# Norm and routing of an expert stage: tokens on the partitions, first maxima by a running count, ranks in bf16

## What is computed

```python
h = rmsnorm(x, g_moe[l])                      # x * rsqrt(mean(x*x) + EPS) * g
g_prob = softmax(xt @ w_rg + b_rg);  p_grp, grp = lax.top_k(g_prob, 1)
e_logits = (xt @ w_re + b_re).reshape(T, N_GROUPS, EXPERTS_PER_GROUP)
e_in = jnp.take_along_axis(e_logits, grp[:, :, None], axis=1)[:, 0]
top_p, top_i = lax.top_k(softmax(e_in), 2)
weights = p_grp * top_p / jnp.sum(top_p, axis=-1, keepdims=True)
hid = silu(xb @ w_gate[e]) * (xb @ w_up[e]);  y = hid @ w_down[e] * w
```

## Time and profile before

| | |
|---|---|
| median of three runs | 1666.05 us |
| the profiled execution | 1660.06 us, its span 1658.3 us |
| granted TensorE clock, mean | 0.944 |
| TensorE busy | 1446.1 us, 87% of the span |
| VectorE busy | 735.5 us, 44% |
| ScalarE busy | 549.2 us, 33% |
| moved from HBM | 371.92 MB, 225 GB/s over the span |

### The profile page before, as it was taken

The page is one execution under the profiler, slowest core; times in us unless marked ns, Lnnn a source line. Parts: engine busy times, 40 slices in busy tenths (PEclk is TensorE's granted clock), DMA queues, the critical chain, the costliest instruction groups (busy, mean ns, idle before and its releaser), DMA issues.

```text
span 1658.3 us, 23155 instructions
## 1 busy us (share of the span) xinstructions
PE 1446.1 (87%) x10239; PEld 1189.1 (72%) x10239; DVE 735.5 (44%) x1072; ACT 549.2 (33%) x678; POOL 2.9 (0%) x8
## 2 busy tenths in 40 slices
PE   7998999877667667576699999999999999999998
PEld 6696888653323223232488888999988888899997
DVE  2555624331101001011487756666466665666642
ACT  2461522311101001001345734444343573453431
POOL 0000000000000000000000000000000000000000
PEclk9997999979988889889899999999999999999999
DMA  6542128449999999999844216556542421655540
GB/s 216 212 175 102 51 102 344 166 165 421 421 421 421 421 421 422 420 421 421 310 153 153 103 53 214 182 163 227 193 163 103 153 102 67 220 171 174 208 153 26
DMA packets 129804, 374.51 MB, mean 226 GB/s; under 512 B 9271, under 2 KB 54631, under 8 KB 105127
## 3 DMA queue, kind: packets, MB, share of 16 engines
q1 hardware_dynamic: 125735, 370.71, 58.7%
q0 software_dynamic: 528, 2.04, 0.4%
q10 hardware_dynamic: 3440, 0.25, 0.2%
HBM read 371.92 MB, written 1.06 MB: 225 GB/s over the span
## 4 chain that ended last, share of the span: by engine, by line
PE 64%; DMA 15%; DVE 9%; SPq 6%; ACT 3%; issue 2%; DVEq 0%; ACTq 0%
PE bank L595 32%; PE bank L1125 7%; DMA ring<-in_w_exp_up 7%; SPq L481 6%; DMA SZ<-in_w_exp_up 5%; PE bank L619 4%; PE bank L951 3%; DVE parts L1576 3%; PE bank L813 3%; PE bank L913 2%; PE bank L641 2%; PE bank L573 2%; PE bank L978 2%; DMA SZ<-in_w_exp_down 2%; DMA ring<-in_w_out 1%
## 5 line engine op out<-in xcount | busy, mean ns | idle before, releaser
L595 PE MATMUL bank<-hnr,parts 128*128 128x256 f32 x4032 | 495.1, 284 | 0.8 <-DVE parts L1576 0.8
L595 PEld LDWEIGHTS bank<-hnr,parts 128*128 128x128 f32 x4032 | 487.9, 192 | 6.1 <-issue 5.1
L1576 DVE TENSOR_TENSOR parts<-ring,parts 128x2048 fp32r<-128x2048 f32 x136 | 306.2, 2287 | 130.8 <-ACT parts L1219 129.2
L1219 ACT ACTIVATE parts<-ring 128x2048 fp32r<-128x2048 f32 x134 | 249.2, 1904 | 156.2 <-DMA ring<-in_w_out 59.5
L951 PE MATMUL bank<-ring,G 128*32 128x512 f32 x768 | 117.1, 766 | 83.1 <-DMA ring<-in_w_exp_up 82.4
L951 PEld LDWEIGHTS bank<-ring,G 128*32 128x32 f32 x768 | 30.6, 135 | 167.5 <-issue 111.2
L1919 DVE COPY SQ<-bank 64x512 f32<-64x512 f32 x16 | 16.7, 1046 | 297.8 <-PE bank L951 297.8
L595 PE MATMUL bank<-SKr,parts 128*128 128x256 f32 x960 | 125.2, 294 | 11.8 <-DVE SKr L1751 9.9
L595 PEld LDWEIGHTS bank<-SKr,parts 128*128 128x128 f32 x960 | 122.7, 202 | 14.5 <-issue 11.2
L1125 PE MATMUL bank<-Gr,parts 128*128 128x256 f32 x640 | 115.3, 283 | 0.0
L1354 ACT ACTIVATE SQ<-bank 64x512 f32<-64x512 f32 x16 | 16.8, 1051 | 267.9 <-PE bank L951 267.9
(11 more groups left out here) (312 smaller groups left out, 1425.1 us busy)
## 6 DMA issues: line engine op xcount, KB each, us to landing
ring<-in_w_in SPq DMA_DIRECT2D x60, 1024.0 KB, 7.3
ring<-in_w_exp_gate SPq DMA_DIRECT2D x48, 1024.0 KB, 26.2
ring<-in_w_exp_up SPq DMA_DIRECT2D x48, 1024.0 KB, 26.5
ring<-in_w_exp_down SPq DMA_DIRECT2D x48, 1024.0 KB, 26.2
ring<-in_w_ffn_in SPq DMA_DIRECT2D x44, 1024.0 KB, 7.6
ring<-in_w_ffn_out SPq DMA_DIRECT2D x20, 1024.0 KB, 6.7
hx<-in_w_exp_gate SPq DMA_DIRECT2D x16, 1024.0 KB, 25.8
SZ<-in_w_exp_up SPq DMA_DIRECT2D x16, 1024.0 KB, 26.7
```

The costliest lines, as they stand in the source:

```text
L595: m = mm(b(name)[:, T * half:T * half + T], part(chunk, ws)[:, k, P * mt:P * mt + P], src[xs][:, k, :], start=k == 0 and i == 0, stop=k == ...
L1219: A(parts[:, 2 * (r % 2), 2048 * i:2048 * i + 2048], ring[:, CHUNK[chunk][0], 2048 * i:2048 * i + 2048], ACT.Copy).then_inc(high_made, 1)
L1576: v.tensor_tensor(parts[:, 2 * (r % 2) + 1, at], ring[:, CHUNK[chunk][0], at], parts[:, 2 * (r % 2), at].bitcast(F32), ALU.subtract).then_ ...
```

## The change

The square sum is made per token on partitions: VectorE adds two of the four double tiles of squares onto the first, and TensorE multiplies 4 x 2 tiles of squares (stationary) with one column of ones, so that the sum, its root and its reciprocal have 2 columns instead of 256. `hn` is no longer normed, only multiplied with the gain, tile by tile as the residual is made. The logits are made with `hn` stationary and the router's weights moving, which gives tokens on partitions at once; six of eight feature tiles stand between and behind the `cw` products. The factor of the token is applied to the logits (L1862 of the changed kernel) and to `htok` as ScalarE's scale. `first_of` uses three instructions (equal, running count by a scan, count is one) in place of five, and works on 32 columns per token for the experts. The mask is bf16 and so are the matrices that count ranks. The accumulators start from the residual between the transposes and the rank. The memsets stand ahead of the residual, and the expert weights `wgt` behind the first `select`. The constants' row of slots counts from one. Its core:

```diff
+for i, name in enumerate(["n_moe", "route"] + [f"ht{i}" for i in range(4)] + ["rank"]):
+    plan[name] = (i % 4, use[i % 4])
+    use[i % 4] += 1
...
-key, wgt, msk = view(KV, 1152, TB, KEYS), view(KV, 1220, TB, NE), view(KV, 1284, TB, NE)
+key, wgt, msk = view(KV, 1152, TB, KEYS), view(KV, 1220, TB, NE), KV[:, 1284:1316].bitcast(BF16)
...
+d4, e4, oh4, same4, nth4, off4 = (small(8 * i, 4) for i in range(6))
+near, near2, same, nth, oh1, oh2 = (small(64 + 64 * i, 32) for i in range(6))
+gm, m1, m2, dm, ex2, pg, w1, w2 = (small(448 + 2 * i, 1) for i in range(8))
+tok_root = sm[:, 84:86]
...
+def route_logits(ks):
+    for k in ks:
+        pe.wait_ge(h_ready, 24 + k + 1)
+        for tb in range(TB):
+            m = mm(b("route")[:, 36 * tb:36 * tb + 36], hn[:, k, P * tb:P * tb + P], wr[:, k, :],
+                   start=k == 0 and tb == 0, stop=k == KT - 1, skip_group_check=True)
+    return m
+def token_sums(ks, first, last):
+    for k in ks:
+        for tb in range(TB):
+            m = mm(b("n_moe")[:, tb:tb + 1], SQ[:, T * k + P * tb:T * k + P * tb + P], ones[:, 0:1],
+                   start=first and k == ks[0] and tb == 0, stop=last and k == ks[-1], skip_group_check=True)
+    return m
+pe.wait_ge(router_in, 64)
+room(pe, "n_moe")
+room(pe, "route")
...
-norm_sum("n_moe")
-pe.wait_ge(router_in, 64)
-room(pe, "routeT")
-for k in range(KT):
-    pe.wait_ge(h_ready, 24 + k + 1)
-    m = mm(b("routeT")[0:36, 0:T], wr[:, k, :], hn[:, k, :], start=k == 0, stop=k == KT - 1)
-fin(m, "routeT")
-emptied(pe, "routeT")
-room(pe, "route")
-for tb in range(TB):
-    m = tr(b("route")[:, 36 * tb:36 * tb + 36], lgT[:, P * tb:P * tb + P], ident[0:36, 0:36])
-fin(m, "route")
+    if j:
+        route_logits((2 * j - 2, 2 * j - 1))
+pe.wait_ge(sq_summed, 2)
+token_sums((0, 1), True, False)
+fin(route_logits((6, 7)), "route")
+pe.wait_ge(sq_ready, 4 * NORMS.index("n_moe") + 4)
+fin(token_sums((6, 7), False, True), "n_moe")
...
+def start_from_residual(tiles):
+    for ft in tiles:
+        mm(ps[4 + ft // 2][:, T * (ft % 2):T * (ft % 2) + T], ident, xres[:, ft, :], start=ft % 2 == 0, stop=False,
+           skip_group_check=True)
+for bank in range(4, 8):
+    pe.wait_ge(bank_free[bank], BEFORE_EXPERTS[bank])
+start_from_residual(range(6))
 pe.wait_ge(mask_ready, 1)
 room(pe, "rank")
-mm(b("rank")[:, 0:32], later, msk[:, 0, :], start=True, stop=True)
-mm(b("rank")[:, 32:64], later, msk[:, 1, :], start=True, stop=False)
-mm(b("rank")[:, 32:64], ones, msk[:, 0, :], start=False, stop=True)
-mm(b("rank")[:, 64:96], ones, msk[:, 0, :], start=True, stop=False)
-m = mm(b("rank")[:, 64:96], ones, msk[:, 1, :], start=False, stop=True)
+mm(b("rank")[:, 0:64], later_b, msk, start=True, stop=False, skip_group_check=True)
+for at in (32, 64):
+    mm(b("rank")[:, at:at + 32], ones_b, msk[:, 0:32], start=False, stop=False, skip_group_check=True)
+m = mm(b("rank")[:, 64:96], ones_b, msk[:, 32:64], start=False, stop=True, skip_group_check=True)
 fin(m, "rank")
-for bank in range(8):
+start_from_residual(range(6, 8))
+for bank in range(4):
     pe.wait_ge(bank_free[bank], BEFORE_EXPERTS[bank])
 pe.wait_ge(blank, 1)
...
-if first:
-    start_from_residual()
-else:
+if not first:
...
 norm_squares("n_moe", xres, [f"cw{j}" for j in range(4)])
-norm_root("n_moe")
+full(act, "n_moe")
+freed(A(tok_root, b("n_moe")[:, 0:TB], ACT.Sqrt, bias=eps_col, scale=1.0 / D), "n_moe")
+act.wait_ge(tok_root_ready, 1)
+for j in range(4):
+    take_permuted(f"ht{j}", htok[:, j // 2, :], 8, j % 2, tok_root[:, j // 2:j // 2 + 1])
 act.wait_ge(route_diff, 1)
 A(e4, d4, ACT.Exp).then_inc(route_exp, 1)
 act.wait_ge(route_diff, 2)
 A(ex2, dm, ACT.Exp).then_inc(route_exp, 1)
-for j in range(4):
-    take_permuted(f"ht{j}", htok[:, j // 2, :], 8, j % 2)
...
-residual([f"cw{j}" for j in range(4)])
+v.memset(zero, 0.0)
+v.memset(ones_b, 1.0)
+v.tensor_copy(later_b, later)
+v.memset(selT, 0.0).then_inc(blank, 1)
+v.memset(key, 0.0)
+v.memset(ahead4, 1.0)
+link(v.memset(ahead, 1.0))
+v.memset(ahead4[:, 0:8:4], 0.0)
+v.memset(ahead[:, 0:64:32], 0.0).then_inc(masks_made, 1)
...
+    residual([f"cw{j}"], j)
...
-norm_apply("n_moe", xres, hn, "g_moe")
+    gain_apply("g_moe", 0, j)
+    if j in (1, 2):
+        dve.wait_ge(sq_ready, 4 * NORMS.index("n_moe") + j + 1)
+        v.tensor_tensor(SQ[:, 0:512], SQ[:, 512 * j:512 * j + 512], SQ[:, 0:512], ALU.add).then_inc(sq_summed, 1)
+        dve.wait_ge(sq_summed, j)
+v.memset(y, 0.0).then_inc(moe_sems[0]["y_out"], 1)
 dve.wait_ge(router_in, 64)
-full(dve, "routeT")
-freed(v.tensor_copy(lgT, b("routeT")[0:36, 0:T]), "routeT")
+dve.wait_ge(masks_made, 1)
+emptied(dve, "n_moe")
+v.reciprocal(tok_root, tok_root).then_inc(tok_root_ready, 1)
+dve.wait_ge(tok_root_ready, 1)
 full(dve, "route")
-freed(v.tensor_tensor(lg, b("route")[:, 0:72].rearrange("p (a c) -> p a c", c=36),
-                      brow.rearrange("p (a c) -> p a c", a=1).to_broadcast([P, TB, 36]), ALU.add), "route")
+for tb in range(TB):
+    last = v.scalar_tensor_tensor(lg[:, tb, :], b("route")[:, 36 * tb:36 * tb + 36], tok_root[:, tb:tb + 1], brow,
+                                  ALU.mult, ALU.add)
+freed(last, "route")
 emptied(dve, "route")
...
-def first_of(dst, value, top, n, t):
-    link(v.tensor_tensor(t, value, bc(top, n), ALU.is_equal))
-    link(v.tensor_scalar(t, t, -100.0, None, ALU.mult))
-    link(v.tensor_tensor(t, t, i100[:, 0:n].rearrange("p (a c) -> p a c", a=1).to_broadcast([P, TB, n]), ALU.add))
-    link(v.tensor_reduce(rmin, t, AX, ALU.min))
-    link(v.tensor_tensor(dst, t, bc(rmin, n), ALU.is_equal))
+def flat(t):
+    return t.rearrange("p a c -> p (a c)")
+def first_of(dst, value, top, n, eq, count, resets):
+    link(v.tensor_tensor(eq, value, bc(top, n), ALU.is_equal))
+    link(v.tensor_tensor_scan(flat(count), resets, flat(eq), 0.0, ALU.mult, ALU.add))
+    return v.scalar_tensor_tensor(dst, count, 1.0, eq, ALU.is_equal, ALU.mult)
...
-first_of(oh4, lg4, gm, 4, t4)
+link(first_of(oh4, lg4, gm, 4, same4, nth4, ahead4))
+link(v.tensor_scalar(off4, oh4, -1.0, BIG, ALU.add, ALU.mult))
 for tb in range(TB):
-    last = v.tensor_tensor(eg[:, tb, :].rearrange("p (g e) -> p g e", g=4),
+    last = v.tensor_tensor(near[:, tb, :].rearrange("p (g e) -> p g e", g=4),
...
-                           oh4[:, tb, :].rearrange("p (g a) -> p g a", a=1).to_broadcast([P, 4, 8]), ALU.mult)
+                           off4[:, tb, :].rearrange("p (g a) -> p g a", a=1).to_broadcast([P, 4, 8]), ALU.add)
...
-for tb in range(TB):
-    last = v.reduce_sum(ein[:, tb, :], eg[:, tb, :].rearrange("p (g e) -> p e g", g=4), AX)
-link(last)
-link(v.reduce_max(m1, ein, AX))
-first_of(oh1, ein, m1, 8, t8)
-link(v.scalar_tensor_tensor(ein2, oh1, -BIG, ein, ALU.mult, ALU.add))
-link(v.reduce_max(m2, ein2, AX))
+link(v.reduce_max(m1, near, AX))
+link(first_of(oh1, near, m1, NE, same, nth, ahead))
+link(v.scalar_tensor_tensor(near2, oh1, -BIG, near, ALU.mult, ALU.add))
+link(v.reduce_max(m2, near2, AX))
...
-first_of(oh2, ein2, m2, 8, t8)
-dve.wait_ge(route_exp, 2)
-link(v.reduce_sum(pg, e4, AX))
-link(v.tensor_scalar(dm, ex2, 1.0, None, ALU.add))
-link(v.tensor_tensor(pg, pg, dm, ALU.mult))
-link(v.reciprocal(w1, pg))
-link(v.tensor_tensor(w2, w1, ex2, ALU.mult))
-link(v.tensor_tensor(t8, oh1, bc(w1, 8), ALU.mult))
-link(v.tensor_tensor(w8, oh2, bc(w2, 8), ALU.mult))
-link(v.tensor_tensor(w8, w8, t8, ALU.add))
-link(v.tensor_tensor(m8, oh1, oh2, ALU.add))
-for dst, s8, s_done in ((wgt, w8, None), (msk, m8, mask_ready)):
-    for tb in range(TB):
-        last = v.tensor_tensor(dst[:, tb, :].rearrange("p (g e) -> p g e", g=4),
-                               oh4[:, tb, :].rearrange("p (g a) -> p g a", a=1).to_broadcast([P, 4, 8]),
-                               s8[:, tb, :].rearrange("p (a e) -> p a e", a=1).to_broadcast([P, 4, 8]), ALU.mult)
-    if s_done is not None:
-        last.then_inc(s_done, 1)
-v.memset(SQ[:, 1324:1644], 0.0)
-v.memset(y, 0.0).then_inc(moe_sems[0]["y_out"], 1)
-v.memset(selT, 0.0).then_inc(blank, 1)
-v.memset(key, 0.0).then_inc(keys_ready, 1)
+link(first_of(oh2, near2, m2, NE, same, nth, ahead))
+v.tensor_tensor(msk, flat(oh1), flat(oh2), ALU.add).then_inc(mask_ready, 1)
+dve.wait_ge(mask_ready, 1)
+full(dve, "rank")
+v.scalar_tensor_tensor(key[:, :, 0:NE], b("rank")[:, 0:64].rearrange("p (a c) -> p a c", c=NE), 1.0,
+                       msk.rearrange("p (a c) -> p a c", c=NE), ALU.add, ALU.mult).then_inc(keys_ready, 1)
...
-full(dve, "rank")
-dve.wait_ge(mask_ready, 1)
-v.scalar_tensor_tensor(key[:, :, 0:NE], b("rank")[:, 0:64].rearrange("p (a c) -> p a c", c=NE), 1.0, msk,
-                       ALU.add, ALU.mult)
-link(v.reduce_max(gm[:, 0, :], b("rank")[:, 64:96], AX))
-freed(v.tensor_copy(cnt[:, :], gm[:, 0, :]), "rank")
-emptied(dve, "rank")
-v.tensor_scalar(key, key, -1.0, None, ALU.add).then_inc(count_ready, 1)
-dve.wait_ge(count_ready, 1)
...
 select(s, 0)
+link(v.reduce_max(gm[:, 0, :], b("rank")[:, 64:96], AX))
```

(12 more changed lines are left out.)

29 lines of the change are left out of this document (10 added, 19 removed).

## The result

| | before | after |
|---|---|---|
| median of the runs made together | 1664.76 us (4 runs, 1662.25 to 1666.34) | 1649.68 us (4 runs, 1645.63 to 1651.45) |
| ratio, 95% interval | | 0.9905 [0.9883, 0.9926] |
| second set of runs, same two kernels | 1665.57 us (13 runs) | 1648.91 us (4 runs), 0.9896 [0.9879, 0.9914] |
| profiled execution (span) | 1660.06 (1658.3) | 1651.45 (1649.6); second set 1649.93 (1648.0) |
| granted TensorE clock, mean | 0.944 | 0.942; second set 0.940 |

The kernel is faster by 15.1 us; 16.8 were forecast, and the time of 1649 is within 0.7 us of both medians. The fills are counted here from one: the prediction's "fill 4" is the fifth.

What follows compares the result with a forecast made beforehand. Bound: the experts' weight stream, 419 GB/s over 438 us, started late by routing. Shorter routing steps move its fill from 362.39 to 345.6, saving 16.8; 1666.05 - 16.8 = 1649.3, taken as 1649 us, own range 1646 to 1653.

Steps and rivals of the forecast that it cites:

- fill 4: Expert weight stream: SP issues this fill at 345.6 instead of 362.39, 16.8 us earlier.
- root, reciprocal, logits: Behind the sums: root 0.2, 0.15 across, reciprocal 0.2, two logit operations 0.4, ending at 331.1.
- first maxima: VectorE up to the mask: 19 instructions in place of 34, 4.4 us, bounds 3.7 and 5.7; mask at 335.5.
- the start of the stream sets the end: Expert stage: one unbroken weight stream, so time saved ahead of its fill at 362.39 moves everything behind it equally.
- Logits and sums: Between and behind the `cw` products: four matmuls cost 0.92 us, bounds 0.5 and 1.8; 3.7 remain behind `cw3`.
- The rank: From mask to `key`: four bf16 matmuls replace five float32 ones, 0.6 us instead of 2.5, bounds 0.2 and 2.5.
- it ends at 334.7, 0.8 before the mask: TensorE finishes transposes (1.97 us) and six accumulator matmuls (2.6 us) in time, so the mask need not wait for it.
- rival 1: Clock falls in logits and sums; TensorE reaches the rank 1.6 us behind the mask; gain 15.2, 1651 us; chance 0.18.
- Gather and `h0`: Between rank and stream: full clock gives 3.7 us for the gather and 3.4 for `h0`, against 7.07 and 5.95.
- rival 2: Gather and `h0` still run at half clock, costing 6.0 us; gain 10.8, 1655 us; chance 0.14.
- its longest rest ahead of the gather is 0.8: TensorE before the gather: rests at most 0.8 us instead of 5, so the gather takes 3.7 us.
- one for one: Whole kernel: the 16.8 us saved ahead of the fill at 362.39 come off the total time in full.

Runs made afterwards that it cites:

- second trace: The changed kernel, unaltered, run and traced once more; ratio 0.9896 against the kernel before, 35.31 us from the `cw` products to the fifth fill.
- the 40 operations: The changed kernel with 40 more small VectorE operations in front of the first maximum; ratio 0.9976 against the kernel before.
- the accumulators twice: The changed kernel with the eight accumulator products made early and repeated behind `h0`; ratio 0.9904 against the kernel before.
- kernel with wide operands: The changed kernel with 108 (72 in the last tile) moving columns in the logits and 128 in the sums; ratio 0.9902 against the kernel before.
- the old layout: The changed kernel with norm and logits of the kernel before, tokens in columns, then turned; ratio 0.9943 against the kernel before.
- the two with early pieces: The changed kernel with wide logits and sums, rank in its own bank, two or three 1 MB pieces of the fifth fill loaded early; 1643.77 and 1642.72 us.
- the kernel with the old maxima: The changed kernel with the five-instruction least-index search and its table `i100` put back; ratio 0.9905 against the kernel before.
- before with the accumulators moved: The kernel before with only the accumulators moved around the rank, and the PSUM banks this needs; ratio 0.9997 against the kernel before.

## Why the prediction was right

| step of the prediction | forecast | after, first trace | second trace |
|---|---|---|---|
| start of `cw` to end of `cw3` | 15.9 | 15.84 | 15.84 |
| rest of logits and sums | 3.7 | 3.32 | 3.33 |
| root, reciprocal, logits | 1.0 | 1.23 | 1.22 |
| first maxima | 4.4 | 4.18 | 4.16 |
| mask to `key` | 0.6 | 1.00 | 1.02 |
| `key` to gather | 1.5 | 1.43 | 1.59 |
| gather | 3.7 | 4.57 | 3.76 |
| `xe` | 0.7 | 0.69 | 0.68 |
| `h0`, and SP | 3.6 | 5.82 | 3.71 |
| sum | 35.1 | 38.08 | 35.31 |

**That the start of the stream sets the end** held among the kernels of after. Eight kernels of the table, from the 40 operations to the accumulators twice, put the fill between 13.0 us behind and 0.6 ahead of where after has it, and the medians followed within 2 us, all of them on the high side, so that the 0.9896 that they are measured from is probably a little low; measured from the 0.9905 of the first set all eight lie within 1.2 us of their fills. The DMA share is 1.01 from 350 to 793 as before. Between before and after the step is weaker: see what stays open.

**Logits and sums** were priced from a row with 64 columns at 0.115 us per record. From one start to the next, eight records took 0.81 to 0.89 us, 0.10 to 0.11 each, with 36 columns as with one, and with 108 or 128 not more than 0.12. So fewer columns hardly lower the price. TensorE's weight loading is busy 2.00 of every 2 us there, so the 128x128 float32 weights may set it; no run has other weights in their place. Against the forecast 0.4 was saved.

**The rank** is the one term that was mis-sized in both traces: 0.6 forecast, 1.0 measured. The bf16 products are not slow (four within 0.37 us in the first trace, 337.25 to 337.62 with the hand-over; 0.43 from mask to `key` where TensorE was free); TensorE was late. The step "it ends at 334.7, 0.8 before the mask" failed: the transposes met the half clock and the accumulators ended at 337.2, 0.6 behind the mask. That is rival 1, at a price of 0.4 to 0.6 instead of its 1.6, since the accumulators ran mostly at full clock again. In the kernel with wide operands TensorE was 0.95 before the mask, as the step had said.

**Gather and `h0`** were forecast at the full clock, 7.4 together, and rival 2 held them at half for 6.0 more. The second trace has 7.47, the first 10.4, because the clock fell at 341.8 in the middle of the gather. So the forecast holds for one execution and half of rival 2 for the other. How often each happens the traces don't say, since only two were recorded; that the medians lie 15.1 and 16.7 below before fits mostly undisturbed ones.

**What was too cheap in the reasoning** is the price of the edits costed at nothing. The accumulators in front of the rank and `wgt` behind the selection were argued as hidden work; "its longest rest ahead of the gather is 0.8" named their effect on the clock in half a sentence. The runs give the price where the cover is gone: 5.7 and 6.9 us, which is as much as the layout (7.4) and far more than maxima and rank (0.3 and 0.8). These sum to 21.1, above the whole 16.5 by which the ways of before and after differ (51.85 - 35.31). Two of them, the 5.7 and the 6.9, are mostly the same loss of clock in gather and `h0`, which can be lost only once; the 7.4 of the layout holds none of it (gather 3.76), but 1.6 of another, in its own product.

**What stays open.** The first pair of traces gives only 8.6 us (1660.06 to 1651.45) where the medians give 15.1. Part is the disturbed gather: the fill moved 12.3 us. Part is the stream, from the fifth fill to the fetch of `w_in`: 438.0 us long before and 443.0 after; behind it after is 1.4 shorter, 856.5 against 857.9. 12.3 - 5.0 + 1.4 is the 8.7 by which the spans differ. The second trace says the same: its fill is 16.1 earlier, its stream 442.5 long, its span only 10.3 shorter. So in both traces the sum's "one for one" gave back 4.5 to 5.0 us for which it has no term. The medians don't show it: the traced execution of before was 4.7 to 5.5 us faster than its medians, for a reason that no run shows. The 16.8 was right at the fill and for its reasons (12.3 and 16.1 in the two traces); that 1649 lies within 0.7 us of both medians is in part luck.

Over all traces the stream is 438.0 in both with the old routing and the old layout, and 439.7 to 443.0 in ten of after and its variants (the two with early pieces apart). Two things are seen in it. One is the rate (last column, GB/s), here in before, in the kernel with the old maxima, and in after:

```profile
380.00:760.00 380.00, 261.24 (x1978) 122.99 (x1970) 43.91 (x143) 34.36 (x53) 0.00 (x0) 0.88 1.01 421
...
380.00:760.00 380.00, 256.44 (x1891) 117.96 (x1891) 41.58 (x133) 32.62 (x49) 0.00 (x0) 0.87 1.01 421
...
380.00:760.00 380.00, 253.63 (x1864) 115.18 (x1860) 40.55 (x132) 32.15 (x49) 0.00 (x0) 0.86 1.01 419
```

It is 421 GB/s in three traces and 419 in the other eleven, which makes 2 us on 438. The three are before, before with the accumulators moved, and after with the old maxima. They are also the three kernels whose table of constants still has the eight columns of `i100` (712 columns wide, 704 in the others), a part of the change for which the prediction has no term. No run changes the width alone, so whether the place of things in memory is the cause stays open. The other is the last `h1`, which waits for its weights and then may find the half clock: 3.64 us in the two kernels with the old routing, 5.0 to 6.6 in the other twelve. Here it is in before and in after, 2.9 us apart:

```profile
796.70 3.64 PE L951 MATMUL bank<-ring,G 128*32 128x512 f32 x32 [2.22 <-DMA ring<-in_w_exp_up]
```
```profile
786.50 6.52 PE L970 MATMUL bank<-ring,G 128*32 128x512 f32 x32 [3.94 <-DMA ring<-in_w_exp_up]
793.09 0.38 SPq L443 DMA_DIRECT2D ring<-in_w_in  x1
```

Rate and last `h1` together are 4.9 of the 5.0 us. A single pair of traces is no measure of the gain here; the intervals of the medians are.

## What to carry to other kernels

Find the transfer that nothing overtakes, ask what its first fill waits for, and price only that chain; whatever moves that fill moved the end one for one here, as long as the stream behind it kept its length: compare that too (438.0 and 443.0). Work laid into the gap in front of a waiting matmul is worth more than its own duration where it keeps the clock up for what follows: ask of each edit "costed at nothing" what the engine would do in its place. Undoing parts one at a time gives numbers that don't add up when several parts protect the same thing.

## What the hardware showed unexpectedly

- The clock fell to its 1.2 GHz level while TensorE never rested: from about 331.6 in after, busy 2.00 of every 2 us, behind 24 products with 36 moving columns or one. With 108 and 128 columns, at nearly the same time per record (0.98 to 1.06 and 1.01 to 1.10 us for eight), it stood at 1.00 in all three kernels built that way, and fell in all eight traces with the narrow ones. The Trainium skill, "TensorE: Matmul & The Clock Gate", Part 1, ties the granted clock to how busy the engine has been. By busy time alone the narrow products should have kept it, and here they did not.
- The gather, 32 records of 64 columns without a pause, ran at the half clock in five kernels, before among them (7.07, 7.06 twice, 6.93, 6.55 us; TensorE had rested 2.3 to 7.5 us ahead of the rank), and did not bring the clock back. In the one with 6.55 it had begun at 1.00 and the clock fell within its first microsecond. Where TensorE had rested 0 to 0.96 us it took 3.76 in eight traces, and 4.57 in the one in which the clock fell within it.
- One and the same kernel had 38.08 and 35.31 us for the same stretch in two executions. A difference of 3 us between two traces around short operands can be the clock and not the code.
- Not tried: the accumulators back behind `h0` with wide logits and sums, the width of the constants by itself, wide products mixed into the gather, and the bank of the rank or the early pieces by themselves.
